# A two-block transformer kernel on one core: small loads, weight splits and the softmax order of the first mixer are moved

## The reference, cut to what matters

```python
def even_mixer(h, w_in, w_out, q_g, k_g, pool_w, pool_scale):
    q, k, v, qi, ki, wi, u = split(h @ w_in)          # 8 query heads, 2 kv heads, index heads, pool input
    q, k = rms_norm(q, q_g), rms_norm(k, k_g)         # per head of 64
    attn = dsa_attention(q, k, v, qi, ki, wi)         # each query keeps the 64 best keys by an index score
    pooled = multiscale_pool(u, pool_w, pool_scale)
    return concatenate([attn, pooled]) @ w_out

def multiscale_pool(u, pool_w, pool_scale):           # 4 groups of 128 channels, windows 2, 4, 8, 16
    mixed = window_mean(u) - u
    y = einsum('btgc,gcd->btgd', mixed, pool_w)
    return y.reshape(b, t, 512) * pool_scale
```

## Time and profile before

| | before |
|---|---|
| median of three runs | 1005.88 us (1004.76 to 1006.89) |
| the profiled execution | 1005.88 us, span of its instructions 1004.0 us |
| PE busy | 985.5 us (98%) |
| DVE busy | 570.9 us (57%) |
| ACT busy | 475.9 us (47%) |
| POOL busy | 44.0 us (4%) |
| granted clock | 1.000 |

### The profile page before, as it was taken

One profiled execution on the slowest core, in us unless ns is written; L12 is line 12 of the kernel. 1 busy time (PEld: TensorE's weight loads), 2 busy tenths in 40 slices (PEclk: granted clock), 3 DMA queues, 4 the chain that ended last, 5 costly groups with the idle time before them and its releaser, 6 DMA issues.

```text
span 1004.0 us, 12665 instructions
## 1 busy us (share of the span) xinstructions
PE 985.5 (98%) x4760; PEld 811.2 (81%) x4760; DVE 570.9 (57%) x630; ACT 475.9 (47%) x519; POOL 44.0 (4%) x59
## 2 busy tenths in 40 slices
PE   6999999999999999999999999999999999999998
PEld 5777888888888888888888888778888888888887
DVE  5777645454474756754544475773465675454443
ACT  5446534343455664644444455455444354444442
POOL 3230000000000000000000012000000000000000
PEclk9999999999999999999999999999999999999999
DMA  8723755565555333655555555445435456555641
GB/s 278 270 98 113 262 172 204 169 206 171 204 188 171 126 126 126 201 197 179 197 177 197 177 189 203 142 145 182 161 128 207 153 187 206 171 205 169 207 167 42
DMA packets 112311, 177.57 MB, mean 177 GB/s; under 512 B 6801, under 2 KB 74513, under 8 KB 112273
## 3 DMA queue, kind: packets, MB, share of 16 engines
q1 hardware_dynamic: 110704, 172.53, 50.7%
q0 software_dynamic: 1280, 3.94, 1.2%
q10 hardware_dynamic: 288, 0.59, 0.2%
HBM read 175.98 MB, written 1.05 MB: 176 GB/s over the span
## 4 chain that ended last, share of the span: by engine, by line
PE 92%; DVE 3%; DMA 2%; POOL 1%; ACT 1%; issue 1%; ACTq 0%; DVEq 0%; POOLq 0%
PE psum L1311 28%; PE psum L1313 28%; PE psum L1312 28%; PE psum L1375 4%; DMA poolw<-in_ev_pool_w 1%; DVE arena L1102 1%; PE psum L1625 1%; DMA cst<-consts 1%; DVE small L1101 1%; POOL head_rs L528 1%; PE psum L1646 1%; PE psum L1408 1%; PE psum L1395 1%; DVE low L907 0%; PE psum L1427 0%
## 5 line engine op out<-in xcount | busy, mean ns | idle before, releaser
L907 DVE TENSOR_TENSOR low<-raw,high 128x2048 fp32r<-128x2048 f32 (+1 forms) x161 | 365.1, 2268 | 300.1 <-ACT high L583 299.7
L583 ACT ACTIVATE high<-raw 128x2048 fp32r<-128x2048 f32 (+1 forms) x163 | 309.1, 1896 | 258.7 <-PE psum L1313 257.3
L1311 PE MATMUL psum<-high,xh 128*128 128x512 f32 x912 | 361.7, 397 | 1.3 <-DVE low L907 1.3
L1313 PE MATMUL psum<-high,xl 128*128 128x512 f32 x912 | 355.9, 390 | 0.0
L1312 PE MATMUL psum<-low,xh 128*128 128x512 f32 x912 | 355.3, 390 | 0.0
L1313 PEld LDWEIGHTS psum<-high,xl 128*128 128x128 f32 x912 | 171.2, 188 | 36.5
L1311 PEld LDWEIGHTS psum<-high,xh 128*128 128x128 f32 x912 | 171.3, 188 | 36.2 <-DVE low L907 1.5
L1312 PEld LDWEIGHTS psum<-low,xh 128*128 128x128 f32 x912 | 171.5, 188 | 33.7
L1311 PE MATMUL psum<-high,gh 128*128 128x512 f32 x240 | 93.6, 390 | 0.0
L1313 PE MATMUL psum<-high,gl 128*128 128x512 f32 x240 | 93.4, 389 | 0.0
L1312 PE MATMUL psum<-low,gh 128*128 128x512 f32 x240 | 93.4, 389 | 0.0
(11 more groups left out here) (147 smaller groups left out, 621.1 us busy)
## 6 DMA issues: line engine op xcount, KB each, us to landing
raw<-in_ffn_w SPq DMA_DIRECT2D x132, 512.0 KB, 4.3
raw<-in_w_in SPq DMA_DIRECT2D x52, 512.0 KB, 4.5
raw<-in_od_w_qkv SPq DMA_DIRECT2D x24, 512.0 KB, 4.5
raw<-in_w_ffn_gate SPq DMA_DIRECT2D x22, 512.0 KB, 3.7
raw<-in_w_ffn_up SPq DMA_DIRECT2D x22, 512.0 KB, 4.7
raw<-in_w_ffn_down SPq DMA_DIRECT2D x22, 512.0 KB, 3.9
raw<-in_ev_w_in SPq DMA_DIRECT2D x12, 512.0 KB, 5.9
raw<-in_ev_w_out SPq DMA_DIRECT2D x8, 512.0 KB, 4.4
```

The lines of the kernel that those rows point to most:

```text
L583: nc.scalar.activation(high[:, n % RING, 0:cols], raw[:, n % RING, 0:cols], ACT.Copy).then_inc(high_ready, 1)
L907: nc.vector.tensor_tensor(low[:, n % RING, 0:cols], raw[:, n % RING, 0:cols], high[:, n % RING, 0:cols].bitcast(F32), ALU.subtract).then_i ...
L1311: nc.tensor.matmul(out, sh, wh, start=start, stop=False, skip_group_check=True)
L1313: return nc.tensor.matmul(out, sl, wh, start=False, stop=stop, skip_group_check=True)
```

## The change: what it does

- The ten small loads move from GpSimd's queue to SP's, between the load of unit 4 and that of the masks. The pool scale is no longer broadcast (`e_scale`); it is loaded as `pool_gain`, one element per partition and group.
- DVE no longer scales `poolw`. The scale is applied where the mixed groups leave PSUM: ACT writes `mh` in four copies with a scale instead of one without, and DVE writes `ml` in four operations instead of one.
- DVE's wait for the small loads and `q_gain` move behind the low part of unit 6. ACT's `split_high(7)` moves behind the two copies of the pooling input.
- The low parts of units 7 and 8 move from GpSimd to DVE: between the two top-k tiles, and after four of the eight rounds of tile 1.
- `query_scale(1)` moves ahead of the low part of unit 9.
- On TensorE `even_pv(0)`, `(1)` and `(2)` stand directly behind `softmax_T` of the same pair.

```diff
 # SP, in the loop over the first units
                 if n == U_POOL:
+                    load_small()          # 8 head gains, pool_gain, poolw, now by sp.dma_start
                     load_consts("causal", "strict", masks_in)
 # GpSimd
             row_rstd(0, 0)
-            load_small()
             load_gain(1, 1)
             head_rstd((0, 1), 2)
-            split_low(U_Q + 1)
-            pool.wait_ge(topk_step, TOPK_SCORED)
-            split_low(U_EOUT)
             head_rstd((2, 3), 8)
 # ACT
-            split_high(7)
             for t in range(NT):
                 copy_chunk(U_POOL, t, e_u[:, t, :], u_copied, 0)
+            split_high(7)
             split_high(8)
...
-            act.wait_ge(poolmix_ready, 1)
-            nc.scalar.activation(mh[:, 4:8, :]..., psum[:, 6:8, :], ACT.Copy).then_inc(poolmix_high, 1)
+            for g in range(4):
+                act.wait_ge(poolmix_ready, 1)
+                nc.scalar.activation(mh[:, 4 + g, :], bank(...), ACT.Copy, scale=pool_gain[:, g:g + 1]).then_inc(poolmix_high, 1)
 # DVE
             split_low(5)
-            dve.wait_ge(small_in, 16 * 10)
-            nc.vector.tensor_scalar(q_gain, head_gain[:, 0:4:2], QK_SCALE, None, ALU.mult).then_inc(q_gain_ready, 1)
-            nc.vector.tensor_tensor(poolw[:], poolw[:], e_scale..., ALU.mult).then_inc(poolw_scaled, 1)
             head_sums((0, 1), 2)
...
             split_low(6)
+            dve.wait_ge(small_in, 16 * 10)
+            nc.vector.tensor_scalar(q_gain, head_gain[:, 0:4:2], QK_SCALE, None, ALU.mult).then_inc(q_gain_ready, 1)
...
             topk_mask(0)
+            split_low(7)
             topk_scores(1)
-            topk_rounds(1, ROUNDS)
+            topk_rounds(1, EARLY_ROUNDS)            # 4
+            split_low(8)
+            topk_rounds(1, ROUNDS - EARLY_ROUNDS)   # 4
             topk_mask(1)
             head_sums((2,), 8)
-            dve.wait_ge(poolmix_high, 1)
-            nc.vector.tensor_tensor(ml[:, 4:8, :]..., psum[:, 6:8, :], mh[:, 4:8, :]..., ALU.subtract).then_inc(poolmix_low, 1)
+            for g in range(4):
+                dve.wait_ge(poolmix_high, 2 * (g // 2) + 2)
+                nc.vector.scalar_tensor_tensor(out=ml[:, 4 + g, :], in0=bank(...), scalar=pool_gain[:, g:g + 1],
+                                               in1=mh[:, 4 + g, :]..., op0=ALU.mult, op1=ALU.subtract).then_inc(poolmix_low, 1)
             query_scale(0)
             head_sums((3,), 8)
-            dve.wait_ge(low_ready, U_EOUT + 1)
+            query_scale(1)
             split_low(9)
-            query_scale(1)
 # TensorE
             def pool_mix():
-                pe.wait_ge(poolw_scaled, 1)
+                pe.wait_ge(small_in, 16 * 10)
...
-            pe.wait_ge(poolmix_low, 1)
+            pe.wait_ge(poolmix_low, 4)
...
             softmax_T(0, 0)
+            even_pv(0)
             tall_quarter(E1, 6, 1, 0, False)
-            even_pv(0)
             even_logits(2)
             softmax_T(0, 1)
+            even_pv(1)
             tall_quarter(E1, 6, 1, 1, False).then_inc(unit_used, 1)
-            even_pv(1)
             even_logits(3)
             softmax_T(0, 2)
+            even_pv(2)
             pe.wait_ge(low_ready, E2 + 1)
+            pe.wait_ge(pv_low, 1)
             tall_quarter(E2, 0, 0, 0, False)
-            even_pv(2)
```

More of the change, by code:

```diff
@@ L216, in program @@
         q_gain = small[:, 188:190]
+        pool_gain = small[:, 190:194]
         row_max = small[:, 194:198].rearrange("p (b t) -> p b t", t=NT)
@@ L270, in program @@
         e_hit = take(SEQ)
-        e_scale = take(512)
         take = Carve()
@@ L329, in program @@
         poolmix_ready, poolmix_high, poolmix_low = sem("poolmix_ready"), sem("poolmix_high"), sem("poolmix_low")
-        poolw_scaled = sem("poolw_scaled")
         logits_ready, max_ready, exp_ready, inv_ready = sem("logits_ready"), sem("max_ready"), sem("exp_ready"), sem("inv_ready")
@@ L424, in pv_bank @@
             return (A_T_BANK, Z_BANK)[p % 2]
-        ROUNDS = N_SEL // 8
-        TOPK_SCORED = IDX_HEADS + 2 * ROUNDS + 1 + IDX_HEADS
         block = ctx.enter_context(nc.Block())
@@ L475, in load_consts, with load_small @@
                 sp.dma_start(cst[:, c0:c1], consts[:, c0:c1]).then_inc(done, 16)
+            def load_small():
+                with nc.allow_non_contiguous_dma(reason="gains of a head: one element per partition"):
+                    for i, g in enumerate((ev_q_norm_g, ev_k_norm_g, q_norm_w_2, k_norm_w_2)):
+                        for r in range(2):
+                            sp.dma_start(head_gain[r * HD:(r + 1) * HD, i:i + 1],
+                                         g[0].rearrange("(p o) -> p o", o=1)).then_inc(small_in, 16)
+                    sp.dma_start(pool_gain, ev_pool_scale[0].rearrange("(g p) -> p g", p=P)).then_inc(small_in, 16)
+                sp.dma_start(poolw[:], ev_pool_w[0].rearrange("g c d -> c g d")).then_inc(small_in, 16)
             early = U_EOUT
@@ L748, in _ @@
             head_square(U_Q, 0, 2, 512, 0)
-            act.wait_ge(poolmix_ready, 1)
-            nc.scalar.activation(mh[:, 4:8, :].rearrange("p (b j) n -> p b (j n)", b=2), psum[:, 6:8, :], ACT.Copy
-                                 ).then_inc(poolmix_high, 1)
+            for g in range(4):
+                act.wait_ge(poolmix_ready, 1)
+                nc.scalar.activation(mh[:, 4 + g, :], bank(6 + g // 2, (g % 2) * SEQ, (g % 2 + 1) * SEQ), ACT.Copy,
+                                     scale=pool_gain[:, g:g + 1]).then_inc(poolmix_high, 1)
             head_square(U_Q, 1, 3, 512, 0)
@@ L1054, in _ @@
             split_low(5)
-            dve.wait_ge(small_in, 16 * 10)
-            nc.vector.tensor_scalar(q_gain, head_gain[:, 0:4:2], QK_SCALE, None, ALU.mult).then_inc(q_gain_ready, 1)
-            nc.vector.tensor_tensor(poolw[:], poolw[:], e_scale.rearrange("p (g d) -> p g d", g=4), ALU.mult).then_inc(poolw_scaled, 1)
             head_sums((0, 1), 2)
@@ L1114, in query_scale @@
                            head_rs[:, 2 + t, :].unsqueeze(2).to_broadcast([P, 8, HD]), 0).then_inc(head_normed, 1)
+            ROUNDS, EARLY_ROUNDS = N_SEL // 8, 4
             topk_scores(0)
@@ L1118, in _ @@
             topk_mask(0)
+            split_low(7)
             topk_scores(1)
-            topk_rounds(1, ROUNDS)
+            topk_rounds(1, EARLY_ROUNDS)
+            split_low(8)
+            topk_rounds(1, ROUNDS - EARLY_ROUNDS)
             topk_mask(1)
             head_sums((2,), 8)
-            dve.wait_ge(poolmix_high, 1)
-            nc.vector.tensor_tensor(ml[:, 4:8, :].rearrange("p (b j) n -> p b (j n)", b=2), psum[:, 6:8, :],
-                                    mh[:, 4:8, :].bitcast(F32).rearrange("p (b j) n -> p b (j n)", b=2), ALU.subtract
-                                    ).then_inc(poolmix_low, 1)
+            for g in range(4):
+                dve.wait_ge(poolmix_high, 2 * (g // 2) + 2)
+                nc.vector.scalar_tensor_tensor(out=ml[:, 4 + g, :], in0=bank(6 + g // 2, (g % 2) * SEQ, (g % 2 + 1) * SEQ),
+                                               scalar=pool_gain[:, g:g + 1], in1=mh[:, 4 + g, :].bitcast(F32),
+                                               op0=ALU.mult, op1=ALU.subtract).then_inc(poolmix_low, 1)
             query_scale(0)
             head_sums((3,), 8)
-            dve.wait_ge(low_ready, U_EOUT + 1)
+            query_scale(1)
             split_low(9)
-            query_scale(1)
             pair_max(0, 0, E_LB)
```

## The result

The change makes the kernel slower: 1011.15 us (1010.56 to 1012.03) against 1005.88 us (1004.76 to 1006.89), both medians of five runs, ratio 1.0056, 95% interval [1.0045, 1.0067]. The profiled execution took 1011.16 us with a span of 1009.3 us, 5.3 us more than the 1004.0 us of before. Forecast were 1007.8 us and a range up to 1010.0: the sign was right, the size was not.

What follows compares the result with a forecast made beforehand. TensorE, busy 98% of the span, was taken as the bound, with DVE tight between 33 and 66 us. A late last E0 quarter (0.4 us) plus the softmax order (1.5) gave 1.9 us over 1005.88: 1007.8 us, range 1006.0 to 1010.0.

Steps and rivals of the forecast that it cites:

- The load wait: Ahead of the index scores: without DVE's wait, scores start at 34.3 us and top-k at 35.8 us, 3.0 us earlier.
- The stall: TensorE ahead of E0: DVE's added low parts and 1.7 us pooled split start E0 near 61.75 us, TensorE standing some 4.4.
- the wait of 0.6 us for `split_high(7)`: DVE between the top-k tiles: tile 0 ends at 43.6 us, the split at 44.1, so DVE idles 0.6 us.
- ACT's four copies: Scaled copies of the pooled result: at most 2.4 us, from 54.6 us, done before DVE asks at 60.0; cost nothing.
- The clock: TensorE's E0 products behind the long stall: counted at the usual 0.23 us apart, with three quarters done at 66.0 us.
- rival B: TensorE after its 4.4 us stall: some 4.2 us of work at half rate, 2.1 us more, 1009.9 us; 22 in 100.
- The loads on SP: Small loads ahead of unit 5: issued at 19.0 us, landing at 24.5 to 26; counted 0, up to 1.5 us.
- rival C: Unit 5 lands late behind the small loads and the top-k starts 1 us late: 1008.8 us; 10 in 100.
- The softmax order: TensorE behind softmax_T waits 0.87 us per pair for ACT's copies, pair 0 absorbed: 1.5 us net, range 0 to 2.6.
- The query scale: Second query transposes: GpSimd's power takes 1.65 instead of 3.63 us, the 1.84 us wait goes; last E0 quarter 0.4 us behind.
- Rival E: Faster: low parts on DVE are hidden and removed waits of 4.4 us are won, E0 at 57.3 us: 1003.5 us; 10 in 100.

Runs made afterwards that it cites:

- a1_filler: Changed kernel with 12 extra TensorE products of 128 x 512 ahead of its wait for the pooled split: 1008.59 us, ratio 1.0036 to the kernel before.
- a4_small_gpsimd: Changed kernel with the ten small loads on GpSimd's queue again, their wait left at its later place: 1010.61 us, ratio 1.0052 to the kernel before.
- c2_best_small: Changed kernel with low parts 7 and 8 on GpSimd, split_high(7) early, old softmax order, small loads on GpSimd's queue: 1001.53 us, ratio 0.9964 to the kernel before.
- a3_low_gpsimd: Changed kernel with the low parts of units 7 and 8 back on GpSimd, split_high(7) still late: 1010.83 us, ratio 1.0057 to the kernel before.
- b2_low_dve: Kernel before with only the low parts of units 7 and 8 moved to DVE: 1010.48 us against 1005.61, ratio 1.0044.
- b3_query_scale: Kernel before with only query_scale(1) moved ahead of the low part of unit 9: 1003.34 us against 1005.61, ratio 0.9972.

## Why the prediction was wrong in size

- **The load wait:** right in kind. The index scores start without a wait, at 34.93 for 34.3 us, and the top-k at 37.05 for 35.8, since unit 5 came late (below).
- **The stall:** right. "It stands for some 4.4 us" measured 4.46; the pooled split 1.65 for the 1.7 taken; E0 at 62.36 for 61.75. That it came so near is in part luck: the top-k began 1.25 us late, and the wait of 0.6 us for `split_high(7)`, which the sum had, fell away for it. ACT's four copies cost nothing, as forecast: they ran from 55.21 to 56.78 us, DVE came at 60.65.
- **The clock:** this step failed. The sum took the products behind the stall at 0.23 us apart and put the lower clock aside as rival B with 22 in 100, since no long stall had been seen inside the work. It is what happens: 14 products followed 0.43 us apart, with a stall of 3.6 us too. Its size of 2.1 us was drawn from the start-up; measured are 2.6 (a1_filler), since the slow stretch lasts 6.1 us in the change. In a3_low_gpsimd it was 3.1 us, so 2.1 lies within what these runs show. The Trainium skill's warning ("TensorE: Matmul & The Clock Gate", Why this matters for your kernels) holds: with it in the sum the forecast would have been 1009.9 us, within 1.3 us of the result.
- **The loads on SP:** priced too low. Their issues took 0.60 us each and not 0.47, so SP came to unit 5 at 20.59 instead of 19.0, and it landed at 27.9 where 24.5 to 26 were estimated. That was rival C, priced at 1.0 us: with a4_small_gpsimd some 0.5 us, within its noise, and 2.1 us where nothing else hides it (c2_best_small).
- **B and C were treated as alternatives.** They have different causes and can come together, and all three occurred: 1.9 + 2.6 + 0.5 = 5.0 of 5.3. The range ended at B alone.
- **The softmax order:** right, 1.5 us, shown both ways. (The rows quoted for a stall of 0.87 us give 80.52 - 79.70 = 0.82.) The records say 0.6 us for each of the three waits, because they count from the modelled end of the last transpose; counted from where the next work would have started, 0.63 us after the transposes' start as before, the second is 84.44 - (82.94 + 0.63) = 0.87.
- **The query scale:** right in mechanism, the power 1.64 us and no wait at the transposes; alone it is worth 2.3 us. The sum credits it with the wait of 1.84 us, which holds only at the full clock: behind the slow products the wait is gone without it (b2_low_dve).
- **Rival E** (the low parts are hidden on DVE) is refuted by b2_low_dve, and so is the thought that GpSimd's low parts slowed the top-k. They left the max and replace operations at their length, and what they held up is the mask with two SBUF inputs that one met in a3_low_gpsimd.

## What to carry to other kernels

Price a stall of TensorE twice, its length and the slow products behind it (1.4 to 2.8 us here), and keep it short before making it rare: here 3.6 us brought the lower clock and 1.9 us did not. Moving elementwise work from an idle engine to the one that feeds TensorE pays only if that engine has slack at this very place; DVE was busy 57% of the span, but had no recorded wait between 33 and 59 us. Add up the side effects of several edits before drawing the range, since they come together. And before moving work on GpSimd in time, look at which DVE operation it will meet.

## What the runs showed of the hardware

- The record of the granted clock reads 1.00 at the start of every profile, and yet the first products run at half rate for a time that differs between executions of the same instructions. Products of 128 x 256 followed 0.12 us apart from 12.67 us on in the profile of before, and 0.21 us apart up to 17.2 us in that of the change. In b3_query_scale, whose instructions up to there are those of the kernel before, they were 0.21 us apart too. The rows are those of the change:

```profile
12.64 0.45 PE L1468 MATMUL psum<-xh,high 128*68 128x256 f32 x1 [0.53 <-DVE xl L906]
12.89 0.41 PE L1469 MATMUL psum<-xh,low 128*68 128x256 f32 x1
...
17.35 0.28 PE L1469 MATMUL psum<-xh,low 128*68 128x256 f32 x1
17.47 0.28 PE L1470 MATMUL psum<-xl,high 128*68 128x256 f32 x1
```

  It shifts TensorE's next steps by some 0.5 us (its transposes of the index queries start at 31.45 us in the change, 30.92 before), since a wait of 1.3 us behind it hides the rest. What decides it was not tried.
- A load of 64 single elements took some 0.6 us to issue on SP and 0.52 on GpSimd (0.64 for the first two), where loads of 512 KB took 0.46 on SP, the median of ten in the change.
